# A two-layer hybrid trunk: a new order of steps, gate rows in memory of their own, quarter-size products, and another division of the opening adaLN work

## The chip, the cores and the metric

The kernel runs on 1 core of one Trainium2 chip. The metric is the device time in microseconds of one launch. Shown is the median of three runs; beside it stands one profiled execution, from which all rows are taken. The engines are TensorE (PE; its weight loads are shown as PEld), VectorE (DVE), ScalarE (ACT), GpSimd (POOL) and SyncE (SP, which here only issues transfers).

## The reference

Two layers work on x of 512 tokens by 1024 channels, batch 1, float32. Cut to what matters here:

```python
mod = silu(c) @ ada_w + ada_b               # 1024 -> 3 x 1024, once per layer
shift, scale, gate = split(mod, 3)
h = rms_norm(x, norm_g) * (1 + scale) + shift
proj = h @ w_in                             # 1024 -> 8008 columns, three mixers and their gates
ya = hgrn2(q, f, i, lower_bound) * silu(hg_g)          # gated linear recurrence, chunks
yb = sparse_attention(q, k, v, indexer) * silu(at_g)   # relu indexer, top 128 of 512 keys
yc = s5(u) * silu(s5_g)                                # complex diagonal scan, GLU
merged = sum_n sigmoid(merge_g[n]) * (y[n] @ w_branch[n])
x = x + gate * (merged @ w_out)             # next layer
```

Within the recurrence the scores of a block of 128 tokens are `q_t . k_s * decay(s, t)` for s before t. The kernel builds them by levels m = 1, 2, 4, ..., 64: level m gives the pairs with s in the first half and t in the second half of a group of 2m tokens.

## The kernel before

Every weight matrix comes in chunks of 128 x 1024 floats (512 KB), 170 of them through a ring `raw` of four slots. A product keeps float32 precision by three fast matmuls (L1687 to L1689): both operands are split in a high part (`w_hi`, `h_hi`, made by ACT, L800 and L860) and a low part (`w_lo` by POOL in two halves, L766 and L767; `h_lo` by DVE, L1359). One chunk is 24 such matmuls of 512 columns. All others (transposes, recurrence levels, attention, column sums) are plain float32, which shows as two records a matmul. `w_hi` and `w_lo` have three slots each, so the split of a chunk waits until PE is through with the chunk three before.

`schedule()` writes one list of steps, STEPS, by hand. Each of the five engines walks the same list and issues its own part of each step, with semaphores between them; an engine never overtakes in its own part. The position of a step in the list is thus its place in five queues. SP looks ahead: at each step it first sends the weight chunks up to three past that step. ACT and POOL look ahead by `split_upto(step)`. PE's list is `tensor_order()`, which puts the column matmuls of adaLN a few chunks later than the step they belong to.

Steps that matter here:

- `xT`, `hs`: x is transposed to channels by tokens, and the mean square of each token is summed over the channels on PE by a matrix of ones (L1770 for layer 0, L1777 for layer 1, in quarters); ACT turns it to `rb`, 1 / rms (L849, L851).
- `ad0`, `ad1`, `md0` (layer 0, four blocks b of 256 channels): the scale part is made on PE as a row (`weight_row`, L1699, one weight column, eight matmuls of 256 columns), copied by ACT to `row` (L827) and turned to columns by PE (`to_columns`, L1706). The shift part is summed on DVE over eight slices (`ada_sum`, L1151 and L1153, each waiting for the one before) and added over partitions by PE with a column of ones (L1742). `md0` adds the bias (L1316, L1317) and makes 1 + scale times norm_g (L1320).
- `hk` (l, b): DVE makes x times scale times rb (L1355), ACT adds the shift and rounds to `h_hi` (L860), DVE makes `h_lo` (L1359). Then `tm iq` b, the first product of the layer (one chunk, 24 matmuls of 512 columns), can run on channels 2b and 2b+1.
- `ada`: 24 half chunks of the modulation of layer 0's gate and of layer 1's scale and shift, summed on DVE (L1153) from three slots in the arena that SP fills one step ahead; PE adds them over partitions (L1763). `mod` finishes them.
- `adp`, `adr`: layer 1's gate as rows on PE (L1699) from two chunks each, 0 and 1 at the border, 2 and 3 among the indexer's steps of layer 1. These eight chunks go through the same ring `raw`, and a slot is free again when PE has used it.
- `hg` (g, part): the recurrence for a pair of heads. Part 0 is the diagonal, parts 1 to 7 the levels (PE L1875; DVE's running products L1504 and its masked copy of the bank into `sct`, L1526), 8 and 9 the chunk states, 10 the output, 11 and 12 the norm. `topk` rounds (L1446, L1449) run on DVE between them.
- `s5`, `s5t`, `gelu`: the S5 branch; in part 2 DVE scans (L1263 to L1277), in part 3 PE turns the result (L1950).
- The border between the layers is the end of the list for layer 0: `wo` products, `hs`, the last `ada`, `adp` 0 and 1, `mod`, then layer 1's `hk`.

The functions that the change touches:

## Time and profile before

| | |
|---|---|
| Median of 3 runs | 1290.11 us (1287.2 to 1292.71) |
| The profiled execution, device time | 1287.9 us |
| Its span | 1286.1 us |
| PE busy | 1250.2 us, 97% |
| PEld busy | 1007.7 us, 78% |
| DVE busy | 870.4 us, 68% |
| ACT busy | 516.5 us, 40% |
| POOL busy | 497.7 us, 39% |
| Mean granted TensorE clock | 0.996 |

Busy time is the time in which at least one instruction of the engine runs. PE's ends are modelled, so back-to-back matmuls overlap in the rows (a 512-column one shows 0.39 us and the next starts 0.23 us later); starts are the numbers to go by. An idle time in square brackets names what ended it.

### The profile page before, as it was taken

The numbers are of one execution on the slowest core, as the hardware profiler recorded it, in microseconds if no ns is written. First come the engines' busy times: TensorE is split into PE (matmuls) and PEld (weight loads), VectorE is DVE, ScalarE is ACT, GpSimd is POOL, SyncE is SP. The second block draws the span as 40 slices with busy tenths as digits, with TensorE's granted clock in tenths as the row PEclk, the third lists the DMA queues.
The fourth block names the chain that finished last, engine by engine and source line by source line (L and its number), as shares of the span: only waits on it lengthen the run. The fifth ranks groups of instructions, "written<-read, shape, count | busy, mean of one in ns | idle before, by whom it ended". The sixth has DMA issues, their size and how long they took to land.

```text
span 1286.1 us, 16449 instructions
## 1 busy us (share of the span) xinstructions
PE 1250.2 (97%) x6240; PEld 1007.7 (78%) x6240; DVE 870.4 (68%) x1364; ACT 516.5 (40%) x858; POOL 497.7 (39%) x344
## 2 busy tenths in 40 slices
PE   7899999999999999999989999999999999999998
PEld 4687788887778878888748767888787888888887
DVE  5777886976587856777478468879656888544242
ACT  5253323763444333333233532256544443433331
POOL 1253243343544333555315322422444434255551
PEclk9999999999999999999989999999999999999999
DMA  9442111132234325473444221212321432244322
GB/s 354 145 162 69 64 53 63 54 127 66 66 92 113 103 75 209 157 254 100 165 158 169 75 107 50 66 52 64 131 66 50 140 99 68 75 150 162 98 82 66
DMA packets 63439, 142.04 MB, mean 110 GB/s; under 512 B 29440, under 2 KB 31616, under 8 KB 62592
## 3 DMA queue, kind: packets, MB, share of 16 engines
q1 hardware_dynamic: 54016, 137.84, 32.8%
q10 hardware_dynamic: 9344, 3.15, 1.0%
q8 instruction: 50, 0.82, 0.3%
q14 instruction: 29, 0.24, 0.1%
HBM read 128.12 MB, written 10.49 MB: 108 GB/s over the span
## 4 chain that ended last, share of the span: by engine, by line
PE 86%; DVE 5%; ACT 3%; DMA 2%; issue 2%; SPq 1%; POOL 0%; ACTq 0%; DVEq 0%
PE bank L1687 22%; PE bank L1689 22%; PE bank L1688 22%; PE bank L1875 4%; DMA raw<-in_wfull 2%; PE bank L1836 2%; PE bank L1860 1%; PE bank L1846 1%; SPq L721 1%; PE bank L1945 1%; PE bank L1699 1%; PE bank L1959 1%; PE bank L1958 1%; DVE h_lo L1359 1%; PE bank L1711 1%
## 5 line engine op out<-in xcount | busy, mean ns | idle before, releaser
L766 POOL TENSOR_TENSOR w_lo<-raw,w_hi 128x512 fp32r<-128x512 f32 (+1 forms) x170 | 241.2, 1419 | 769.0 <-ACT w_hi L800 769.0
L1687 PE MATMUL bank<-h_hi,w_hi 128*128 128x512 f32 x896 | 363.0, 405 | 2.1 <-ACT arena L874 2.1
L1689 PE MATMUL bank<-h_hi,w_lo 128*128 128x512 f32 x896 | 349.5, 390 | 0.0
L1688 PE MATMUL bank<-h_lo,w_hi 128*128 128x512 f32 x896 | 348.8, 389 | 0.0
L800 ACT ACTIVATE w_hi<-raw 128x1024 fp32r<-128x1024 f32 (+2 forms) x170 | 178.4, 1052 | 266.3 <-PE bank L1689 205.7
L767 POOL TENSOR_TENSOR w_lo<-raw,w_hi 128x512 fp32r<-128x512 f32 (+2 forms) x170 | 264.0, 1553 | 0.0
L1687 PEld LDWEIGHTS bank<-h_hi,w_hi 128*128 128x128 f32 x896 | 168.3, 188 | 42.9 <-issue 8.3
L1688 PEld LDWEIGHTS bank<-h_lo,w_hi 128*128 128x128 f32 x896 | 168.4, 188 | 38.7 <-issue 5.3
L1689 PEld LDWEIGHTS bank<-h_hi,w_lo 128*128 128x128 f32 x896 | 168.1, 188 | 35.8
L1687 PE MATMUL bank<-w_hi,h_hi 128*128 128x512 f32 (+1 forms) x256 | 97.6, 381 | 8.1 <-DVE h_lo L1359 4.4
L1688 PE MATMUL bank<-w_lo,h_hi 128*128 128x512 f32 (+1 forms) x256 | 95.3, 372 | 0.0
L1689 PE MATMUL bank<-w_hi,h_lo 128*128 128x512 f32 (+1 forms) x256 | 95.2, 372 | 0.0
L1687 PE MATMUL bank<-y_hi,w_hi 128*128 128x512 f32 x224 | 89.0, 397 | 0.0
L1689 PE MATMUL bank<-y_hi,w_lo 128*128 128x512 f32 x224 | 87.3, 390 | 0.0
L1688 PE MATMUL bank<-y_lo,w_hi 128*128 128x512 f32 x224 | 87.2, 389 | 0.0
L1153 DVE SCALAR_TENSOR_TENSOR ada<-arena,cs,ada 128x256 f32<-128x256 f32 x112 | 79.7, 711 | 6.4 <-DMA arena<-in_wada 2.5
L1875 PEld LDWEIGHTS bank<-arena 128*128 128x128 f32 x512 | 60.2, 192 | 10.5 <-issue 9.2
L1504 DVE TENSOR_TENSOR arena<-arena 128x1024 f32<-128x1024 f32 x28 | 45.5, 1625 | 31.0 <-PE bank L1875 30.9
L1875 PE MATMUL bank<-arena 128*128 128x128 f32 x512 | 63.0, 278 | 1.4 <-ACT arena L903 1.4
L1687 PEld LDWEIGHTS bank<-w_hi,h_hi 128*128 128x128 f32 x256 | 48.5, 189 | 18.3 <-issue 9.6
L1689 PEld LDWEIGHTS bank<-w_hi,h_lo 128*128 128x128 f32 x256 | 48.4, 189 | 7.8
L1688 PEld LDWEIGHTS bank<-w_lo,h_hi 128*128 128x128 f32 x256 | 48.6, 190 | 7.0
(276 smaller groups left out, 1797.8 us busy)
## 6 DMA issues: line engine op xcount, KB each, us to landing
raw<-in_wfull SPq DMA_DIRECT2D x178, 512.0 KB, 3.6
arena<-in_wada SPq DMA_DIRECT2D x40, 512.0 KB, 6.7
x_scratch<-xm SPq DMA_DIRECT2D x2, 2048.0 KB, 8.4
arena<-x_scratch SPq DMA_DIRECT2D x2, 2048.0 KB, 9.5
arena<-in_x SPq DMA_DIRECT2D x4, 512.0 KB, 5.6
arena<-in_s5m SPq DMA_DIRECT2D x2, 1024.0 KB, 6.4
u_scratch<-arena ACTq DMA_DIRECT2D x4, 512.0 KB, 4.0
arena<-u_scratch SPq DMA_DIRECT2D x8, 256.0 KB, 3.3
```

The source lines that it names most:

```text
L721: sp.dma_start(mt2[j % 2][jj * GC:(jj + 1) * GC, :, jj * GC:P], kt[0:GC, :, 0:(CH - jj) * GC]).then_inc(mt_in, 16)
L766: nc.gpsimd.tensor_tensor(lo[:, :half], raw_chunk(n)[:, :half], hi[:, :half].bitcast(F32), ALU.subtract)
L767: nc.gpsimd.tensor_tensor(lo[:, half:], raw_chunk(n)[:, half:], hi[:, half:].bitcast(F32), ALU.subtract).then_inc(lo_done, 1)
L800: nc.scalar.activation(chunk_view(n, w_hi[:, m % SPLIT_SLOTS]), raw_chunk(n), ACT.Copy).then_inc(hi_done, 1)
L1153: ins = v.scalar_tensor_tensor(acc, weights_[:, kk], c_k, acc, ALU.mult, ALU.add)
L1359: v.scalar_tensor_tensor(h_lo[:, k], ht[:, k % 4], mod[:, l, k:k + 1], h_hi[:, k].bitcast(F32), ALU.add, ALU.subtract).then_inc(h_ready, 1)
L1504: return v.tensor_tensor(qk, qk, ends.broadcast_to([P, 2, S // m, m]), ALU.mult)
L1687: mm(out_, a_hi, b_hi, start=first, stop=False)
L1688: mm(out_, a_hi, b_lo, start=False, stop=False)
L1689: return mm(out_, a_lo, b_hi, start=False, stop=last)
L1836: mm(dst[:, 0:(b + 1) * P], iq_t[ps, h // 2, b * P:(b + 1) * P], ik_t[ps, 0:(b + 1) * P], start=True, stop=True).then_inc(full((step, 0)), 1)
L1875: last = mm(dst[:, cs_], hk[:, 2 * g + i, cs_], hq[:, 2 * g + i, cs_], start=True, stop=True)
```

## The change

The list of steps is new from end to end, and so are these parts:

- Begin of layer 0: DVE sums the scale (`mac`) in two accumulators in turn, one for each half of the input channels, in place in the loaded tiles; PE adds both over partitions (four column matmuls, `ad1`). PE makes the shift as a row (`ad0`), ACT copies it at the new step `adc`, PE turns it to columns. ACT's `h_hi` waits for the shift, DVE adds it after its two products. DVE makes the low parts of the first four chunks (`low`); POOL begins with the fifth. ACT's Sin for the rope tables moves from `ad0` 0 to `ad0` 2. SP sends the scale tiles ahead of the shift tiles, and masks, gains and S5 vectors after the fourth block, not the third.
- Layer 1's gate rows: the eight tiles are loaded into `gate_home` in the arena by a new SP step `gin`, no longer through `raw`; `adp` 0, 1 and 2 stand at the border, 3 at the begin of layer 1.
- The column matmuls and the loads of `ada` are steps of their own (`adm`, `adl`), and `tensor_order()` is gone.
- The last level of the recurrence (m = 64) is a 64 x 64 product per block of 128 instead of 128 x 128, and DVE copies that quarter instead of a masked copy of the whole.

The diff, cut to its core (of the new order only the lines that the prediction speaks of):

```diff
-    steps += [("hs", 0), ("ad0", 0), ("ad1", 0)]
+    steps += [("hs", 0), ("ad0", 0), ("mac", 0), ("low", 0), ("ad1", 0), ("adc", 0)]
...
-            steps += [("md0", 0), ("hk", 0, 0), ("ad0", 1)] + tm("iq", 0) + [("ad1", 1), ("md0", 1), ("hk", 0, 1), ("ad0", 2)]
-            steps += tm("iq", 1) + [("ad1", 2), ("md0", 2), ("hk", 0, 2), ("ad0", 3)] + tm("iq", 2)
-            steps += [("ad1", 3), ("md0", 3), ("hk", 0, 3), ("lb", 0), ("s5l", 0, 0)] + tm("iq", 3)
+            steps += [("md0", 0), ("hk", 0, 0), ("ad0", 1), ("mac", 1), ("low", 1)] + tm("iq", 0)
+            steps += [("ad1", 1), ("md0", 1), ("adc", 1), ("hk", 0, 1), ("ad0", 2), ("mac", 2), ("low", 2), ("mac", 3)] + tm("iq", 1)
+            steps += [("ad1", 2), ("md0", 2), ("adc", 2), ("hk", 0, 2), ("ad0", 3), ("ad1", 3), ("md0", 3), ("low", 3), ("adc", 3)] + tm("iq", 2)
+            steps += [("hk", 0, 3), ("lb", 0), ("s5l", 0, 0)] + tm("iq", 3)
...
-        steps += cm("wo", 3, 0) + cm("wo", 2, 1) + next_layer("hs", 1) + cm("wo", 3, 1) + more(1) + out_tiles(1, 0, 1) + more(5)
-        steps += next_layer("hs", 2) + next_layer("adp", 0) + next_layer("hs", 3) + next_layer("mod", 0) + next_layer("adp", 1)
+        steps += cm("wo", 2, 1) + rows(1) + more(1) + cm("wo", 3, 1) + next_layer("adp", 0) + fetch(2) + rows(2) + next_layer("hs", 1)
+        steps += more(1) + fetch(1) + out_tiles(1, 0) + more(4) + next_layer("adp", 1) + fetch(1) + next_layer("adp", 2) + rows(2)
+        steps += out_tiles(1, 1) + out_tiles(2, 0) + more(1) + next_layer("hs", 2, 3) + out_tiles(2, 1) + rows(1) + out_tiles(3, 0, 1)
+        steps += next_layer("mod", 0) + fetch(1)
...
+        steps += late("adp", 3) + rope("iq0") + rope("iq1") + late("adr", 0) + tm("kvi", 0) + rope("ik") + [("s5l", l, 1)] + late("adr", 1)
...
+        steps += hg(0, 9, 10) + hg(1, 8) + cm("hg", 0, 0) + top1(11) + rope("qn") + top1(12, 13) + hg(0, 11) + top1(14) + top(2) + top1(15)
+        steps += rope("qs") + hg(0, 12) + cm("hg", 0, 1) + hg(1, 9, 10) + gate("hg", 0, 0) + cm("hg", 1, 0) + rope("q0") + rope("q1")
...
+                if kind == "gin":
+                    p = step[2]
+                    sp.wait_ge(y_done, gate_no(l - 1, 2, 3) + 1)
+                    if p == 3:
+                        sp.wait_ge(mt_in, 16 * CH * NW * l)
+                    for kh in range(2):
+                        sp.dma_start(gate_home[2 * p + kh], wada[16 + len(ADA) + 2 * GATE_ROWS.index((l, p)) + kh].rearrange(
+                            "p (k w) -> p k w", k=KC)).then_inc(gate_in[p], 16)
...
+                if kind == "mac":
+                    b = step[1]
+                    dve.wait_ge(scale_in[b], 32)
+                    halves = [ad_in[4 * b + 2 + kh] for kh in range(2)]
+                    done = []
+                    for kk in range(KC):
+                        for kh in range(2):
+                            acc = halves[kh][:, 0]
+                            c_k = cs[:, 2, KC * kh + kk:KC * kh + kk + 1]
+                            if kk == 0:
+                                done.append(mark(v.tensor_scalar(acc, acc, c_k, None, ALU.mult)))
+                                continue
+                            after(done[2 * (kk - 1) + kh])
+                            ins = v.scalar_tensor_tensor(acc, halves[kh][:, kk], c_k, acc, ALU.mult, ALU.add)
...
+                if kind == "low":
+                    b = step[1]
+                    dve.wait_ge(hi_done, b + 1)
+                    v.tensor_tensor(chunk_view(b, w_lo[:, b % SPLIT_SLOTS]), raw_chunk(b),
+                                    chunk_view(b, w_hi[:, b % SPLIT_SLOTS]).bitcast(F32), ALU.subtract).then_inc(lo_done, 1)
...
-                    act.wait_ge(mod_ready, b + 1 if l == 0 else 4 + l)
+                    if l == 0:
+                        wait_read(act, (("adc", b), 0))
+                    else:
+                        act.wait_ge(mod_ready, l)
...
+                            if m == P // 2:
+                                half = [a.rearrange("p (c t) -> p c t", c=NT)[0:P // 2, :, P // 2:]
+                                        for a in (sct[:, 2 * g + i], banks[i][:])]
+                                v.tensor_copy(*half).then_inc(read((step, i)), 1)
+                                return
...
+                                if part == len(LEVELS):
+                                    first, second = slice(c * P, c * P + P // 2), slice(c * P + P // 2, (c + 1) * P)
+                                    last = mm(dst[0:P // 2, second], hk[:, 2 * g + i, first], hq[:, 2 * g + i, second],
+                                              start=True, stop=True)
+                                    continue
```

## Rows read from the trace of the kernel before

**Rows 1.** the page, busy time, share of the span and instructions

```profile
span 1286.1 us, 16449 instructions
...
PE 1250.2 (97%) x6240; PEld 1007.7 (78%) x6240; DVE 870.4 (68%) x1364; ACT 516.5 (40%) x858; POOL 497.7 (39%) x344
```

**Rows 2.** 25 us stretches: PE, PEld, DVE, ACT, POOL busy, clock, DMA, GB/s

```profile
50.00:75.00 25.00, 20.55 (x101) 17.57 (x102) 21.15 (x46) 8.64 (x14) 9.45 (x8) 0.93 0.35 127
...
650.00:675.00 25.00, 19.23 (x73) 10.32 (x73) 20.61 (x35) 10.32 (x14) 6.25 (x4) 0.86 0.58 200
...
875.00:900.00 25.00, 24.76 (x128) 20.35 (x127) 24.57 (x47) 14.53 (x20) 5.93 (x6) 1.00 0.22 64
```

**Rows 3.** waits of PE over the span: us, times, longest

```profile
PE bank L1763 <- DVE ada L1153: 5.2, 2, 4.3
...
PE bank L1950 <- DVE arena L1276: 3.7, 2, 2.2
...
PE bank L1687 <- ACT arena L881: 1.6, 2, 0.8
```

**Rows 4.** timeline of PE at the begin: start, us, then the instruction

```profile
29.00 0.47 PE L1687 MATMUL bank<-w_hi,h_hi 128*128 128x512 f32 x1 [0.72 <-DVE h_lo L1359]
...
39.44 0.47 PE L1687 MATMUL bank<-w_hi,h_hi 128*128 128x512 f32 x1
...
60.31 0.77 PE L1687 MATMUL bank<-w_hi,h_hi 128*128 128x512 f32 x1 [3.67 <-DVE h_lo L1359]
```

**Rows 5.** timeline of DVE at the begin

```profile
19.12 3.61 DVE L1153 SCALAR_TENSOR_TENSOR ada<-arena,cs,ada 128x256 f32<-128x256 f32 x7
...
25.83 1.42 DVE L1355 SCALAR_TENSOR_TENSOR arena<-xm,mod,arena 128x512 f32<-128x512 f32 x2
...
29.15 5.50 DVE L1153 SCALAR_TENSOR_TENSOR ada<-arena,cs,ada 128x256 f32<-128x256 f32 x7
```

**Rows 6.** timeline of POOL at the begin

```profile
29.04 1.29 POOL L766 TENSOR_TENSOR w_lo<-raw,w_hi 128x512 fp32r<-128x512 f32 x1 [3.26 <-ACT w_hi L800]
```

**Rows 7.** groups of DVE: busy, mean ns, idle before and releaser

```profile
L1504 DVE TENSOR_TENSOR arena<-arena 128x1024 f32<-128x1024 f32 x28 | 45.5, 1625 | 31.0 <-PE bank L1875 30.9
...
L1516 DVE TENSOR_TENSOR arena<-arena 128x1024 f32<-128x1024 f32 x4 | 4.9, 1222 | 0.1
```

**Rows 8.** timeline of PE at the border between the layers

```profile
650.30 3.61 PE L1699 MATMUL bank<-raw,cs 128*1 128x256 f32 x16
...
653.85 1.98 PE L1777 MATMUL bank<-arena,cst 128*128 128x512 f32 x4
...
661.94 1.01 PE L1763 MATMUL bank<-cst,ada 128*128 128x1 f32 x4 [4.25 <-DVE ada L1153]
...
662.88 6.00 PE L1699 MATMUL bank<-raw,cs 128*1 128x256 f32 x16
...
669.49 0.47 PE L1687 MATMUL bank<-w_hi,h_hi 128*128 128x512 f32 x1 [0.61 <-issue]
...
681.98 0.50 PE L1687 MATMUL bank<-w_hi,h_hi 128*128 128x512 f32 x1 [1.33 <-POOL w_lo L767]
```

**Rows 9.** timelines of ACT and DVE at the border

```profile
656.57 1.28 ACT L851 ACT_TABLE_LOAD   x1
...
663.15 1.06 ACT L800 ACTIVATE w_hi<-raw 128x1024 fp32r<-128x1024 f32 x1 [4.65 <-DMA raw<-in_wfull]
...
666.08 3.31 DVE L1359 SCALAR_TENSOR_TENSOR h_lo<-arena,mod,h_hi 128x512 fp32r<-128x512 f32 x2 [1.27 <-ACT h_hi L860]
```

**Rows 10.** timeline of PE, small plain products

```profile
168.16 2.05 PE L1875 MATMUL bank<-arena 128*128 128x128 f32 x16
...
466.95 3.74 PE L1945 MATMUL bank<-arena 128*128 128x64 f32 x32
```

**Rows 11.** groups of weight loads, by form

```profile
L1875 PEld LDWEIGHTS bank<-arena 128*128 128x128 f32 x512 | 60.2, 192 | 10.5 <-issue 9.2
...
L1929 PEld LDWEIGHTS bank<-arena 128*16 128x16 f32 x128 | 11.8, 97 | 4.2 <-issue 2.8
```

More of the change, by code:

```diff
@@ L70, in schedule, with taken, fetch, rows @@
         todo += [("ada", l + 1, c) for c in range(16)] if l + 1 < DEPTH else []
-        if todo:
-            todo.insert(12, ("mod", l, 16))
-        def more(n):
-            out = []
-            while todo and (n or todo[0][0] == "mod"):
-                n -= todo[0][0] == "ada"
-                out.append(todo.pop(0))
-            return out
+        fetches = [("adl", l, i) for i in range(len(todo))]
+        columns = [("adm", l, p) for p in range(len(todo) // 2)]
+        def taken(from_, n):
+            out = from_[:n]
+            del from_[:n]
+            return out
+        def more(n):
+            return taken(todo, n)
+        def fetch(n):
+            return taken(fetches, n)
+        def rows(n):
+            return taken(columns, n)
+        def first_gates():
+            return [("mod", 0, 16)] if l == 0 else []
         def tm(name, *cs_):
@@ new lines, in schedule @@
+        steps += load("yback", 2) + s5(3, 2) + tab(3, 3) + cm("wb1", 2) + s5(3, 3) + gelu(2, 0) + gelu(1, 1) + gelu(2, 1)
+        steps += cm("mg1", 3) + s5(3, 4) + load("ysave", 3) + fetch(2) + more(2) + gelu(0, 2, 3) + fetch(1) + cm("wb1", 3)
+        steps += cm("sg", 0, 0) + load("yback", 3) + more(1) + gelu(1, 2, 3) + cm("sg", 0, 1) + cm("sg", 1, 0) + gelu(3, 0) + gelu(2, 2)
+        steps += cm("sg", 1, 1) + gelu(2, 3) + gelu(3, 1, 2) + cm("mg2", 0, 0) + fetch(2) + more(1) + fetch(2) + more(1) + rows(1)
@@ L184, in chunks_of @@
     kind = step[0]
-    if kind == "adp":
-        return [ada_chunk(step[1], 16 + 2 * step[2] + kh) for kh in range(2)]
     if kind == "tm":
@@ L268, in done_after @@
     for step in STEPS:
-        if step[0] != "adp":
-            n += len(chunks_of(step))
+        n += len(chunks_of(step))
         done[step] = done[group_of(step)] = n
@@ L390, in split_upto @@
         return 0
-    if step[0] in ("ad0", "ad1", "md0", "hk") and DONE[step] < 4:
-        return DONE[step] + (step[0] != "ad0")
-    if step[:3] == ("tm", 0, "iq"):
-        return DONE[step] + 1
-    if step[0] == "hk" and step[1] or step[0] == "adp" and step[2] < 2 or step[0] == "hs" and step[2] > 1:
-        return DONE[step] + (step[0] == "hk" and step[2] > 0)
+    if step[0] == "low":
+        return step[1] + 1
+    if DONE[step] <= 4 and step[0] in ("ad0", "mac", "adc", "ad1", "md0", "hk"):
+        return 0
+    if step[:3] == ("tm", 0, "iq") and step[3] < 3:
+        return 0
     near = FIRST[step] + len(chunks_of(step)) + RAW_SLOTS
-    return min(DONE[step] + (3 if step[0] in ("gelu", "s5", "s5t") else 2), sum(n < near for n in SPLIT_CHUNK))
-SHIFTS = (0, 1, 2, 3)
+    return min(DONE[step] + (3 if step[0] in ("gelu", "s5", "s5t") else 2), near, len(CHUNKS))
 WARM = 8
-ADP_NO = {n: i for i, n in enumerate(n for n in range(len(CHUNKS)) if n not in SPLIT_NO)}
+FIRST_LOW = 4
 def program(nc, wfull, wada, x, cvec, pos, lblog, vecs, gains, s5v, s5m, consts, masks, out):
@@ L547, in program @@
         ad0_acc, adp_used = sem("ad0_acc"), sem("adp_used")
+        gate_in = [sem(f"gate{p}_in") for p in range(4)]
         shift_in = [sem(f"shift{b}_in") for b in range(4)]
@@ L677, in _ @@
             for b in range(4):
-                for i in range(4):
+                for i in (2, 3, 0, 1):
                     if 4 * b + i == 15:
```

226 lines of the change are left out of this document (92 added, 134 removed).

## The prediction

> **What bounds the kernel now.** First the page's busy shares and span: TensorE (PE) is busy 1250.2 of 1286.1 us, so all its idle time together is 35.9 us; DVE, the next, is busy 68% [rows 1]. The kernel gets faster only where PE has less to do, where a PE wait goes, or where PE's clock doesn't fall. Then busy time in stretches of 25 us: PE loses 4.5 us in 50:75 and 5.8 us in 650:675, each time at a lower granted clock (0.93, 0.86) [rows 2]; these are the start of layer 0 and the border between the layers. Last, the waits by PE: on DVE's adaLN sums 5.2 us, on DVE in the S5 scan 3.7 us, on ACT's bank copies 1.6 us [rows 3]. What is left is thin: DVE is at 24.6 of 25 us in 875:900 while PE still loses only 0.2 us there [rows 2].
>
> **The change, part by part, against the profiled execution (span 1286.1, device time 1287.9 us).**
>
> *Begin of layer 0.* Before, the four blocks b go in one rhythm: 24 matmuls of iq (5.5 us), then PE's adaLN work for the next block, then iq again; it starts at 29.00 and 39.44, a period of 10.44 us, which also holds a PE-made row of 3.6 us [rows 4]. The fourth block has no further row to hide behind, so PE waits 3.67 us and starts at 60.31 at the low clock; 25 us at a mean of 0.93 are 3.5 us at half speed, 1.7 us of work lost, part of it in the idle time itself, so I take 1.4 [rows 2, 4]. The last iq matmul is thus over at about 60.3 + 5.5 + 1.4 = 67.2.
> DVE's sum over eight slices is one dependent chain: 7 instructions take 3.61 us when alone (0.52 each with the semaphore), but 5.50 us when POOL makes a low part [rows 5]; POOL's first half stands at 29.04, exactly there [rows 6]. So a POOL low part costs DVE 1.9 us. After the change POOL makes none of the first four. DVE makes each itself, one 128x1024 instruction of 1.22 us (the row of that size, undisturbed) [rows 7], and its sum runs in two independent accumulators. A chained instruction costs 0.52; two independent ones 512 wide take 1.42 together, 0.7 each [rows 5], so one 256 wide is worth 0.35 to 0.52; I take 0.40, sum 3.1 us (ends 2.6 and 4.0).
> Now the clock of the new order. Block 0: sum 18.8 to 21.9, low part to 23.1; PE's row is over at 23.0, the four column matmuls at 23.9; scale 24.4, two products to 25.8, the shift added 25.95, ACT's high parts to 27.3, h_lo to 28.1: iq starts at 28.2 instead of 29.0. Block 1: DVE has sum and low part done at 28.1 + 3.1 + 1.2 = 32.4, PE finishes iq at 33.7 and the columns at 34.6; from there the chain is 4.4 us (0.4 scale, 1.4 products, 0.2 shift, 1.4 high, 0.8 low, 0.2 semaphores), while PE has row and columns of 4.1 us to do: iq at 39.0. The chain is 0.3 us longer than before, because ACT now waits for the shift. Block 2: DVE has two sums and one low part in the one window, 39.0 + 3.1 + 1.2 + 3.1 = 46.4, 1.8 us later than PE has the columns (44.5 + 0.9 less overlap); h_lo at 50.6; PE meanwhile makes the row for block 3, and its columns wait for ACT's copy, which stands behind a high part (1.06): iq at 51.9 instead of 49.9. Block 3 then has everything ready: iq at 57.4 with no wait and no low clock, over at 62.9. The gain is 67.2 - 62.9 = 4.3, taken as **-4.5** with rounding of the first step; with the slow sum (4.0) it is -2.7, with the fast one -5.3. ACT's two Sin and their table load move to block 2, where ACT has 5 us free. SP's queue sends scale before shift; both land in the same place in turn as before, and masks, gains and S5 vectors now wait for the last block's four loads, with nothing needing them before 56 us.
>
> *Border.* Before: last wo matmul 647.6, first iq matmul 669.49. In between PE makes two sums of squares (1.9 each), two gate rows (3.61, and 6.00 at the low clock) and waits 4.25 us for DVE's last adaLN sum [rows 8]. Then the high parts wait for weights, since the gate rows sit in the raw ring (ACT idle 4.65 us on DMA raw), and POOL's low parts fall on DVE's h_lo: two take 3.31 us, where two undisturbed ones of this size take 1.4 [rows 5, 9]. After the change the gate rows have memory of their own, so iq's first two chunks are split during the wo matmuls. But the gap gets more PE work: adp 0, 1, 2 (3 x 3.6), hs 1, 2, 3 (1.9 each), four column steps (0.5 each): 18.5 us, ending 666.1. These now end last: ACT's Ln and Exp around a table load of 1.28, 2.7 us -> 668.8 [rows 9], and 3.2 us from there to the first matmul (as 25.83 to 29.00 in block 0) -> 672.0 [rows 4, 5]. DVE's last two sums wait for a column step that stands behind adp 2 (661.7) and end at 665.7, below the other chain. PE is idle 5 us, so the low clock comes again: +1.5 -> 673.5. Moved in from elsewhere are hs 1 and adp 2, 1.9 + 3.6 = 5.5; net 668.0 against 669.5, -1.5. The wait on POOL at 681.98 (1.33) [rows 8] goes, because PE arrives later than POOL. adp 3 between iq and kvi covers layer 1's half of the wait for ACT's bank copies, 0.8 us [rows 3]. Together -3.6; taken **-3.5**. Ends: 0 (the row work ends last and the low clock lasts through a whole chunk) and -5 (no low clock).
>
> *Quarter products.* The last level of each head pair runs 64x64 instead of 128x128: 2 layers x 2 pairs x 2 heads x 4 chunks = 32 matmuls, 64 records, all on the PE path. A 128x128 record costs 0.112 us: 16 take 2.05 with the last one's tail; one with 64 moving columns but 128 weight columns costs the same (32 in 3.74) [rows 10]. So the moving side doesn't count, the weight load does. No row has 64 weight columns. A load of 16 takes 97 ns, one of 128 takes 192 [rows 11]; between them 64 comes to 131, 0.68 of 192, which makes 0.076 per record and -2.3 us. Ends: 0 (no gain) and half the time, -3.6, or -5 if 64 by 64 is cheaper still than either half. I take **-2.5**.
> The Trainium skill, "TensorE: Matmul & The Clock Gate", section "LDWEIGHTS (loading the stationary operand)", has the load go with the number of weight columns alone, columns divided by 1.2 in ns; as an estimate that is 53 ns less per record, -3.4 us, and a total of 1278.7. That 64 moving columns cost as much as 128 under 128 weight columns agrees with it.
> DVE's eight masked copies become plain ones of a quarter's size: that takes time off DVE only, 0 on the path.
>
> *The new order inside the layers.* SP's, ACT's, DVE's and PE's orders all move. Work is the same. PE's waits between 75 and 640 us and between 710 and 1125 are small, and 3.7 us of them are the S5 scan's [rows 3], where wb1's third chunk still is the only cover and DVE still waits for ACT's sine; gelu's sigmoid ahead of it costs ACT 0.6. Relu runs of five are broken up, which can give 1 to 2 us. On the other side recurrence parts 9 and 10 now follow each other directly on PE in both pairs. Taken **0**, ends -4 and +8.
>
> Sum: -4.5 - 3.5 - 2.5 + 0 = -10.5, so 1277.4 for an execution like the profiled one (1287.9), which lies 2.2 below the median of the runs shown (1290.1); on that median 1279.6. I give 1279.5.
>
> **Rivals.**
> A, DVE takes the place (1279.6 + 8 = 1287.6). With parts 9 and 10 adjacent, PE waits for states that DVE makes only after level 7's product (1.63 us [rows 7]) and copies: about 2 us at 4 places, +8. For it: DVE at 24.6 of 25 [rows 2]. Against: DVE waited 30.9 us for PE ahead of the 28 level products [rows 7], 1.1 us each, so it runs ahead of PE.
> B, the edits don't do what they say (1287.9). The slices of the sum stay at 0.52 and DVE's three jobs in block 2's window end last (-2.7), the border's 18.5 us of PE work with a long low clock costs 4 more (-3.5 + 4 = +0.5), and a quarter product costs what a whole one does (0). For: 6.00 against 3.61 for the same row of eight matmuls [rows 8]. Against: chunks split early save 1.9 us of DVE.
> C, the other side (1299). The new order puts DVE behind PE by more than the 1.1 us it is now ahead at the 28 level products; from that point each place makes PE wait. At 0.7 us a place beyond the slack it is 28 x 0.7 = +20: 1279.6 + 20 = 1299.6. For: the masked rounds of top-k are spread anew between the levels. Against: PE loses 0.2 us in DVE's fullest window [rows 2], and low parts and masked copies lighten DVE.
>
> **How the numbers follow.** Forecast 0.62, A 0.22, B 0.07, C 0.09. The forecast's own range is 1273 to 1284. The range given, 1271 to 1290, takes in A and B and the ends of begin, border and quarter products; C is left out. No change is within 0.5% (6.5 us), about what can be told here: 1283.6 to 1296.6. Faster 0.65, same 0.26, slower 0.09.
>
> **What would show it.** Right: iq starts near 28.2, 39, 52 and 57.4 with no wait and a clock of 1.0 in 50:75; no POOL work before 56; six adaLN sums after the last wo; first iq matmul of layer 1 at about 18 us behind hs 1, PE idle about 5 us before it, no POOL wait after; 64x64 records at 0.06 to 0.08. Wrong: PE waits above 1 us at the recurrence's state product or the level products, a level record still at 0.112, or a fourth iq start past 60.

## The result, and the profile after

The kernel after takes 1269.2 us (median of 4 runs, 1268.4 to 1269.9), the one before 1291.4 (4 runs, 1287.2 to 1292.7); the ratio is 0.983 [0.9813, 0.9846]. That is 22 us faster, where 10.5 were forecast, and below the range given. The profiled execution after has a span of 1268.1 us (device time 1269.9) against 1286.1 (1287.9), so the two traces account for 18.0 of the 22. Of the other 4.2, 3.5 come from the profiled execution before, which is at the fast end of its kernel: of 62 timed runs (medians by group 1289.4 to 1291.4) one lies below it. The begin below shows one reason. The last 0.8 is that the profiled execution after is the longest of its four. All medians here leave out three executions (1826 and 4473 us of `quarter_alone`, 7197 of `mtin3_earlier`); the 1.7 us that an expectation below names for `quarter_alone` counts two of them in.

The page after, busy time of the engines (to compare with [rows 1]). PE is idle for 21.2 us, where it was 35.9.

```profile
PE 1246.9 (98%) x6256; PEld 1006.5 (79%) x6256; DVE 847.7 (67%) x1368; ACT 518.4 (41%) x860; POOL 479.6 (38%) x336
```

Stretches of 25 us, columns as in [rows 2]: the low clock is gone at the begin and still there at the border.

```profile
50.00:75.00 25.00, 24.22 (x136) 21.14 (x135) 21.86 (x44) 12.81 (x20) 8.31 (x7) 1.00 0.48 169
650.00:675.00 25.00, 19.52 (x73) 13.75 (x72) 15.13 (x26) 12.38 (x16) 4.67 (x4) 0.86 0.25 84
475.00:500.00 25.00, 25.00 (x128) 21.29 (x127) 11.21 (x19) 9.29 (x12) 8.46 (x7) 1.00 0.48 168
```

PE's waits over the span of the kernel after, the largest first. Of [rows 3] the adaLN sums (5.2) and the S5 scan (3.7) are gone; a wait of 5.5 with no releaser is new, the border's. The one of 1.1 for w_lo lies in layer 0.

```profile
PE bank L1714 <- DMA lbt<-in_lblog: 5.8, 1, 5.8
PE bank L1691 <- issue: 5.5, 1, 5.5
PE bank L1691 <- POOL w_lo L747: 1.1, 1, 1.1
PE bank L1691 <- ACT arena L856: 1.1, 1, 1.1
PE bank L1691 <- ACT arena L863: 0.8, 1, 0.8
...
PE bank L1910 <- DVE arena L1528: 0.5, 2, 0.3
```

Since work moved between places, equal times of two traces don't compare. What compares is the time between the starts of the same weight chunks on PE, worked out from PE's timeline of each profile (us; L0, L1 the layer; wb0 is the start of attention, mg1 means its first chunk, with which the S5 part begins here, and wb1 3 the fourth chunk of wb1, behind it; the columns between before and after are experiments from below, their names cut short):

```
from - to                     before  quart_a middle_a  mtin3_l  old_mid  mtin3_e    after
first matmul - L0 kvi          62.96    65.16    64.49    64.48    58.82    59.07    58.83
L0 kvi - wb0 (recurrence)     198.94   197.98   199.96   198.92   197.86   197.84   197.88
L0 wb0 - mg1 (attention)      127.27   127.22   125.95   127.39   127.26   125.95   125.95
L0 mg1 - wb1 3 (S5)            99.41   101.03    96.86    96.99    99.50   100.56    96.86
L0 wb1 3 - last wo            147.79   147.67   147.80   148.29   147.26   146.42   146.42
last wo - L1 hq 1             124.72   125.47   127.22   125.34   120.11   122.97   122.93
L1 hq 1 - wb0                 138.07   137.04   136.70   138.09   137.03   134.87   134.86
L1 wb0 - mg1 (attention)      127.18   126.93   125.95   131.41   127.45   125.95   125.95
L1 mg1 - wb1 3 (S5)            98.71    98.88    96.89    98.33    99.95    98.58    96.86
L1 wb1 3 - end                150.76   150.76   150.89   150.77   150.76   150.89   150.89
```

From before to after: begin -4.1, S5 -2.6 and -1.8, attention -1.3 and -1.2. The four rows that are left (L0 kvi to wb0, wb1 3 to the last wo, from there to hq 1, hq 1 to wb0) make -7.4 together, of which 2.1 are the quarter products (below).

*Begin.* PE of the kernel after, the starts of iq's four chunks; and DVE while PE works on the second of them (a sum is one row of 2 and one of 6, the low part stands behind it; the fourth block's sum follows at 44.42 in the same form).

```profile
29.82 0.47 PE L1691 MATMUL bank<-w_hi,h_hi 128*128 128x512 f32 x1 [0.25 <-DVE h_lo L1358]
...
40.62 0.47 PE L1691 MATMUL bank<-w_hi,h_hi 128*128 128x512 f32 x1 [0.25 <-DVE h_lo L1358]
...
52.63 0.50 PE L1691 MATMUL bank<-w_hi,h_hi 128*128 128x512 f32 x1
...
58.20 0.39 PE L1691 MATMUL bank<-w_hi,h_hi 128*128 128x512 f32 x1
```
```profile
40.39 0.61 DVE L1294 TENSOR_SCALAR arena<-arena,cs 128x256 f32<-128x256 f32 x2
40.91 2.46 DVE L1297 SCALAR_TENSOR_TENSOR arena<-arena,cs 128x256 f32<-128x256 f32 x6
43.29 1.22 DVE L1305 TENSOR_TENSOR w_lo<-raw,w_hi 128x1024 fp32r<-128x1024 f32 x1
```

A sum takes 2.9 us (40.39 to 43.29; forecast 3.1), the fourth chunk follows the third without a wait, and kvi starts at 64.58.

*Border.* PE of the kernel after, from the last wo product:

```profile
637.32 3.61 PE L1702 MATMUL bank<-arena,cs 128*1 128x256 f32 x16
640.86 1.05 PE L1763 MATMUL bank<-cst,ada 128*128 128x1 f32 x8
641.77 1.96 PE L1777 MATMUL bank<-arena,cst 128*128 128x512 f32 x4
643.67 7.07 PE L1702 MATMUL bank<-arena,cs 128*1 128x256 f32 x32
650.66 1.05 PE L1763 MATMUL bank<-cst,ada 128*128 128x1 f32 x8
651.58 3.87 PE L1777 MATMUL bank<-arena,cst 128*128 128x512 f32 x8
655.36 0.61 PE L1763 MATMUL bank<-cst,ada 128*128 128x1 f32 x4
661.45 0.77 PE L1691 MATMUL bank<-w_hi,h_hi 128*128 128x512 f32 x1 [5.48 <-issue]
```

This is the forecast's chain: 18.5 us of PE work were expected and are there, then a wait (5 forecast, 5.5 measured), and the low clock (records of 0.63 us until 666.7, 0.39 after).

*Quarter products.* A group of 16 takes 1.15 us, where [rows 10] have 2.05. The kernel after, and the same place with full-size products (`full_last_level`, below):

```profile
212.16 1.15 PE L1877 MATMUL bank<-arena 128*64 128x64 f32 x16
213.23 1.60 PE L1898 MATMUL bank<-arena 128*128 128x128 f32 x12
```
```profile
212.43 1.95 PE L1870 MATMUL bank<-arena 128*128 128x128 f32 x16
214.21 1.50 PE L1888 MATMUL bank<-arena 128*128 128x128 f32 x12
```

By the starts, a quarter record follows the one before after 0.058 us instead of 0.112. But each group of 16 pays at its edges: its first record starts 0.32 us behind the one ahead of it (0.23 at full size), what follows it starts 0.15 behind its last (0.11), and the next one 0.21 behind that (0.11). A group thus saves 0.5 us and not 16 x 0.054 = 0.9; the four groups save 2.1 us.

### The profile page after: what moved, and what is told of

Read it like the earlier page. It is cut to its first block, busy times and chain, and to the rows that moved or that the text cites. A ratio compares the mean times of both kernels' runs of the same rounds, so it can differ in the third digit from the quotient of the medians.

```text
span 1268.1 us, 16483 instructions
## 1 busy us (share of the span) xinstructions
PE 1246.9 (98%) x6256; PEld 1006.5 (79%) x6256; DVE 847.7 (67%) x1368; ACT 518.4 (41%) x860; POOL 479.6 (38%) x336
## 4 chain that ended last, share of the span: by engine, by line
PE 95%; DVE 2%; issue 1%; ACT 1%; POOL 1%; DMA 0%; SPq 0%; ACTq 0%; DVEq 0%
PE bank L1691 24%; PE bank L1693 24%; PE bank L1692 24%; PE bank L1880 4%; PE bank L1950 2%; PE bank L1836 2%; PE bank L1702 2%; PE bank L1846 1%; PE bank L1860 1%; PE bank L1934 1%; PE bank L1964 1%; PE bank L1963 1%; PE bank L1714 1%; PE bank L1853 1%; PE bank L1941 1%
## 5 line engine op out<-in xcount | busy, mean ns | idle before, releaser
L746 POOL TENSOR_TENSOR w_lo<-raw,w_hi 128x512 fp32r<-128x512 f32 (+1 forms) x166 | 235.7, 1420 | 769.1 <-ACT w_hi L780 769.0
L747 POOL TENSOR_TENSOR w_lo<-raw,w_hi 128x512 fp32r<-128x512 f32 (+2 forms) x166 | 251.2, 1513 | 0.0
L1691 PEld LDWEIGHTS bank<-w_hi,h_hi 128*128 128x128 f32 x256 | 48.8, 190 | 18.4 <-issue 11.2
L1503 DVE TENSOR_TENSOR arena<-arena 128x1024 f32<-128x1024 f32 x28 | 38.1, 1360 | 37.1 <-PE bank L1880 18.7
L1880 PEld LDWEIGHTS bank<-arena 128*128 128x128 f32 x448 | 52.2, 192 | 6.7 <-issue 5.9
L1135 DVE SCALAR_TENSOR_TENSOR ada<-arena,cs,ada 128x256 f32<-128x256 f32 x84 | 51.7, 615 | 5.1 <-DMA arena<-in_wada 2.4
L1880 PE MATMUL bank<-arena 128*128 128x128 f32 x448 | 54.5, 278 | 0.0
```

The source lines that it names most:

```text
L746: nc.gpsimd.tensor_tensor(lo[:, :half], raw_chunk(n)[:, :half], hi[:, :half].bitcast(F32), ALU.subtract)
L747: nc.gpsimd.tensor_tensor(lo[:, half:], raw_chunk(n)[:, half:], hi[:, half:].bitcast(F32), ALU.subtract).then_inc(lo_done, 1)
L1135: ins = v.scalar_tensor_tensor(acc, weights_[:, kk], c_k, acc, ALU.mult, ALU.add)
L1503: return v.tensor_tensor(qk, qk, ends.broadcast_to([P, 2, S // m, m]), ALU.mult)
L1691: mm(out_, a_hi, b_hi, start=first, stop=False)
L1880: last = mm(dst[:, cs_], hk[:, 2 * g + i, cs_], hq[:, 2 * g + i, cs_], start=True, stop=True)
```

## The experiments

All times are medians; what is compared with the kernel after is compared with its 1269.2, from four runs. The kernel before, timed again in each group of experiments, moved by 2 us between the groups, so a difference to 1269.2 of less than that is shown only where the stages show it too.

**The middle alone, and put back.** `middle_alone`: the kernel before with

```
- kvi 0, ropes, kvi 1, adr 0, kvi 2, ... idx(1, 3), adp 2, ... mg1 3 1   (old order)
+ iq ropes, kvi 0, ik rope, kvi 1, adr 0, kvi 2, ... mg1 3              (new order, adp and adr as before)
```


> The kernel before with one part of the change alone: the new order of the steps between the iq product and the last chunk of mg1, in both layers (adp 2, adp 3 and the adr steps stay where they stood, in the middle). Theory 1: the forecast's term of 0 for the new order was the failed step; the gaps between TensorE's matmuls beyond their back-to-back time fall by about 5 us in the middle of layer 0 and by about 8 in that of layer 1, so this kernel is 8 to 12 us faster than before, near 1281. The two S5 waits behind L1950<-DVE (3.7 us before) are gone. Rival 2: the term of 0 was right and the gain came from begin, border and products, which are each larger than forecast: this kernel is within 2 us of before. Rival A of the forecast, recurrence parts 9 and 10 adjacent: a PE wait of about 2 us at four places, 8 us slower.

Measured 1285.7 us, ratio to before 0.9958 [0.9946, 0.997]: 5.2 faster, less than expected. In its profile both S5 waits are gone, attention is shorter by 1.3 and 1.2, and the recurrence of layer 0 is 1.0 us longer: PE's first output product of a head pair (part 10) waits for DVE's masked copy of the last level's scores. The new order has no weight chunk between the two (waits of PE):

```profile
PE bank L1906 <- DVE arena L1527: 2.0, 4, 0.8
```

`old_middle`: the kernel after with the old order there.

> The kernel after with the old order between kvi and the last chunk of mg1 put back (adp 3, adr 0 and adr 1 stay ahead of and behind kvi 0, as in the kernel after). Theory 1: it gives back what the new middle brought: 8 to 12 us slower than after, near 1279, ratio to before 0.991. Rival 2 (the middle is worth nothing): within 2 us of after, 0.983.

Measured 1280.5 us: 11.3 slower than after. So the new order is worth 5.2 in the old surroundings and 11.3 in the new: theory 1, and the forecast's 0 is refuted from both sides. The stages of the two profiles differ by 8.6 us only. Of the 6 us between 5.2 and 11.3 the quarter copies explain 1.5 (below), and PE's S5 waits, 5.3 us here against 3.7 before, about as much; the rest is open. Rival A's place is the right one, its price 2.0 us instead of 8; what PE waits for there is the copy of the last level, not the chunk states.

**The place of mtin 3.** `mtin3_later` (before) and `mtin3_earlier` (after) are the same move in opposite directions:

```
  before: ... s5(3, 1) + load("mtin", 3, 0, 1) + cm("mg1", 2, 1) + tab(3, 2) + s5(2, 4) ...
  after:  ... s5(3, 1) + cm("mg1", 2, 1) + tab(3, 2) + s5(2, 4) + load("mtin", 3, 0, 1) ...
```


> The kernel before with one move: the eight transfers of mtin 3 on SP's queue stand behind chunk mg1 2 1 and S5 part 4 of block 2 instead of ahead of it, as in the kernel after. Theory 1: these transfers held up the weight chunks behind them, so ACT's high part, its Sin table and DVE's states came late; both S5 waits of PE (2.4 and 1.3 us, one in each layer) go, 2.5 to 3.7 us faster than before. Rival: the wait belongs to the order of gelu and tables on ACT, which stays here: within 1 us of before, and the waits stand.

> The kernel after with one move undone: the eight transfers of mtin 3 stand on SP's queue ahead of chunk mg1 2 1 again, where the kernel before had them; all else stays. In the kernel before, the opposite move alone brought 4.3 us by the medians and took both waits of PE for S5's states away. Theory: the place of these transfers is the whole of the S5 waits, so they come back (2.4 us in layer 0, 1.7 to 2.9 in layer 1), 4 to 5 us slower than after, near 1273.8. Rival: the new order around it (table parts and sigmoid in other places) has given ACT and DVE enough room of its own, so that it is within 1 us of after; then the gain of the order in the kernel after has several roots.

Measured: `mtin3_later` 1286.6 us, 4.3 faster than before, ratio 0.9969 [0.9959, 0.998]; `mtin3_earlier` 1275.3 us, 6.1 slower than after. The place of the eight small transfers on SP's queue is the largest part of what the forecast missed. The chain in the kernel before, first SP, then ACT (L1006 is the Sin for the S5 states):

```profile
460.51 5.09 SPq L721 DMA_DIRECT2D arena<-arena  x8
465.64 0.59 SPq L673 DMA_DIRECT2D raw<-in_wfull  x1
```
```profile
470.18 1.06 ACT L800 ACTIVATE w_hi<-raw 128x1024 fp32r<-128x1024 f32 x1 [5.46 <-DMA raw<-in_wfull]
```

The same in `mtin3_earlier`:

```profile
453.55 5.08 SPq L701 DMA_DIRECT2D arena<-arena  x8
458.67 0.97 SPq L647 DMA_DIRECT2D raw<-in_wfull  x1
```
```profile
462.92 1.06 ACT L780 ACTIVATE w_hi<-raw 128x1024 fp32r<-128x1024 f32 x1 [4.56 <-DMA raw<-in_wfull]
...
465.00 1.28 ACT L988 ACT_TABLE_LOAD   x1
466.29 0.63 ACT L988 ACTIVATE arena<-arena 128x512 f32<-128x512 f32 x1
```

SP has sent nothing since 439.9: it waits 13.5 us for ACT to make what the eight transfers carry, then takes 5.1 us to issue the eight. The weight chunk behind them is sent at 458.7; in the kernel after it is sent at 440.8, ahead of them. ACT waits 4.6 us for it, and the Sin for the S5 states (L988) stands behind that high part in ACT's queue. In the kernel after the same rows are, SP first:

```profile
454.56 5.95 SPq L701 DMA_DIRECT2D arena<-arena  x8
461.70 0.33 SPq L705 DMA_DIRECT2D y_scratch<-arena  x1
```
```profile
458.54 1.06 ACT L780 ACTIVATE w_hi<-raw 128x1024 fp32r<-128x1024 f32 x1
...
463.51 0.63 ACT L988 ACTIVATE arena<-arena 128x512 f32<-128x512 f32 x1
```

No weight chunk stands behind the eight, the high part starts without a wait, and the Sin is 2.8 us earlier. PE's wait is then 0 instead of (waits of PE in `mtin3_earlier`, and 10 us of the same kernel; columns as in [rows 2])

```profile
PE bank L1955 <- DVE arena L1258: 3.3, 2, 1.8
```
```profile
470.00:480.00 10.00, 8.31 (x28) 6.23 (x29) 9.30 (x13) 3.53 (x5) 3.06 (x2) 0.83 0.31 116
```

The clock fell too. The stage S5 of layer 0 is 3.7 us longer (table), of layer 1 1.7, together 5.4 of the 6.1. In the profile of `mtin3_later` both old S5 waits are gone, but it is the longest of its twelve runs (1292.0): it has a wait of 4.0 us for another S5 state, in the attention row of layer 1 (131.4 us). ACT waits 8.0 us there for a weight chunk sent among two groups of four such transfers; the kernel before sends them at the same moments and waits 5.1. `old_middle` has 0.4 us of PE's wait at this place, the other profiles have none; why the chunk landed later stays open.

**The quarter products in both orders.** `quarter_alone` (before with them), `full_last_level` (after without them); q and k stand for the operands:

```
+ if part == len(LEVELS):  mm(dst[0:64, second], k[.., first], q[.., second])     # PE
+ if m == P // 2:          v.tensor_copy(*half)                                      # DVE
```


> The kernel before with the quarter products alone (TensorE 64 by 64, and DVE's plain copy of the quarter). All theories: 64 records at a spacing of 0.058 us as in the kernel after, where they took 0.112; 64 x 0.054 = 3.5 us faster than before. Theory 1 (the middle was mis-sized, the rest right): 3.5, ratio 0.997. Rival 2 (each of the other parts larger than forecast): 5 or more, as DVE's shorter copies also take PE's small waits away. If DVE then is late at the next level instead: under 2.

> The kernel after with the last level of the recurrence at full size again (128 by 128 on TensorE, the masked copy on DVE), in the new order. Quarter products alone gave 1.7 us to the kernel before by the medians, and in its profile only 1.0 of the 1.73 us of each layer. Theory 1, the part and the order need each other: in the new order the product of the state (recurrence part 11) stands directly behind, and DVE's full masked copies are late for it: 3.5 us for the records, and 0.5 to 1 us of waits at four places, 4 to 6 us slower than after, 1273.5 to 1275. Rival, both are worth the same in either order: 1.7 to 2.5 slower than after.

Measured: `quarter_alone` 1288.5 us, 2.4 faster, ratio 0.9981 [0.9971, 0.999]; `full_last_level` 1272.4, 3.2 slower than after. In the old order the recurrence shrinks by 1.0 us a layer, which is two groups at 0.5 us, so the 3.5 that all theories took was too much; in the new it shrinks by 1.8, the two groups and 0.7 of waiting. Without the quarter copies the output product waits as in `middle_alone` (here L1900, 2.0 us in four waits; after 0.5 in two):

```profile
PE bank L1900 <- DVE arena L1525: 2.0, 4, 0.8
```

So the two parts need each other, as theory 1 has it: the smaller copies save 1.5 us, but only in the new order. Its 4 to 6 us were too high, because it took the records at 3.5 instead of 2.1.

**Attention.** `old_attention`: after, with the old order from mg0 0 0 to su 1 1.

> The kernel after with the old order of attention, top-k rounds and su around chunks mg0 0 0 to su 1 1, all before and behind it as in the kernel after. With the whole old middle, this stage took 127.3 and 127.5 us instead of 125.95 (from wb0's first chunk to mg1 1 0). Theory: six stalls of 0.4 to 0.5 us of PE on ACT's and DVE's parts of attention in each layer come back, 1.3 to 1.5 a layer: 2.5 to 3 us slower than after, 1272. The S5 stage stays at 96.9 us. Rival: the S5 stage is disturbed as well, since att and tables stand differently: 4 or more.

Measured 1271.4 us, 2.2 slower. Attention is 0.9 and 1.2 us longer, S5 unchanged. The 2.5 to 3 expected were a little high. PE waits for ACT's part of attention again (L1861, 1.0 us in three); which move within the stage takes the waits away was not taken apart.

**The begin.** `low_on_pool` and `halves_one_by_one` each undo one way of making the sum shorter, `sum3_later` the place of the fourth sum:

```
low_on_pool:        - dve: v.tensor_tensor(w_lo, raw, w_hi, subtract)      + pool: the same in two halves
halves_one_by_one:  - for kk in range(KC): for kh in range(2):              + for kh in range(2): for kk in range(KC):
sum3_later:         - ("low", 2), ("mac", 3)] + tm("iq", 1)                + ("low", 2)] + tm("iq", 1) ... ("mac", 3), ("low", 3)] + tm("iq", 2)
                    (and ad1 3, md0 3, adc 3 behind iq's third chunk instead of ahead of it)
```


> The kernel after with the first four low parts made by POOL again, in two halves each, instead of by DVE. The forecast's reason (a low part on POOL slows a DVE sum that runs beside it, 1.9 us a sum of seven instructions): DVE saves 1.2 us a block but loses about as much or more in each sum; blocks 0 and 1 start 1 to 2 us later, 1 to 4 us slower than after in all. Rival, that slowing is covered by PE's own row and iq work from block 1 on: within 1 us of after; then DVE's taking over the low parts is worth nothing.

> The kernel after with the two halves of each scale sum one after the other instead of in turn: each instruction of DVE then waits for the one just before it. If the forecast's 0.52 us for a chained instruction and 0.40 for one in turn hold, each sum is 0.8 to 1 us longer; block 0 starts that much later, and block 2, where two sums and a low part stand in one window, 1.6 to 2 later: 2.4 to 3 us slower than after. Rival, the chain's waits cost nothing at 256 wide: within 0.5 us.

> The kernel after with the fourth block's scale sum, low part, columns and shift one window later: they stand ahead of and behind iq's third chunk, as the second block's stand around the first, instead of being made in the third block's window. Theory (the forecast's point): the fourth block then has no row of its own to hide behind, so PE waits about 3 to 4 us ahead of iq's fourth chunk and the granted clock falls; against it iq's third chunk can start earlier, by up to 1.2 us: 3 to 5 us slower than after, near 1273. Rival: the third window was too full (two sums and a low part), and it comes out within 1 us: then the gain of the begin lies in something else.

Measured: 1269.8, 1271.5 and 1274.9 us: 0.6, 2.3 and 5.7 slower than after. With POOL at its side, the second block's sum takes 5.0 us instead of 2.9 (DVE in `low_on_pool`, while PE works on the first chunk):

```profile
29.49 1.64 DVE L1292 TENSOR_SCALAR arena<-arena,cs 128x256 f32<-128x256 f32 x2
31.06 3.49 DVE L1295 SCALAR_TENSOR_TENSOR arena<-arena,cs 128x256 f32<-128x256 f32 x6
```

But DVE is then through at 34.5 and PE at 36. While PE works on the second chunk it is POOL that waits: the two sums take 2.9 us each, and POOL's instruction 4.67 instead of 1.3. The begin is 0.8 us longer by the stages; so the rival is right and the low parts are worth nearly nothing. With the halves one by one a sum takes 3.7 us, as expected; blocks 0 and 1 lose nothing by it, the third chunk comes 1.3 us later, and the begin is 1.2 us longer in the profile (the shortest of its runs). What counts is the fourth block. PE in `sum3_later`, and its stretch:

```profile
62.00 0.76 PE L1691 MATMUL bank<-w_hi,h_hi 128*128 128x512 f32 x1 [3.80 <-DVE h_lo L1358]
```
```profile
50.00:75.00 25.00, 20.16 (x94) 16.56 (x93) 20.13 (x46) 9.87 (x17) 6.91 (x6) 0.86 0.40 148
```

The same wait is in every kernel with the old begin, and in three of four it has this clock of 0.86; the profile before had 0.93 [rows 2]. This is one place where that execution was lucky: iq's first chunk to kvi took 39.3 us in it, 39.8 to 40.4 in the three others.

**The border, towards a faster version.** Seven kernels move adp 2, adp 3 and the two adr steps of the kernel after:

```
adp3_in_gap:          + adp 3 ahead of mod                       - adp 3 behind iq
adp3_gap_adr_iq:      the same, adr 0 behind iq 1, adr 1 behind iq 3
adp2_behind_squares:  adp 1, column, hs 2, hs 3, 2 columns, adp 2    - adp 1, adp 2, 2 columns, hs 2, hs 3, column
adp2_behind_adr0_iq:  the same, adr 0 behind iq 1
adp2_between:         adp 1, column, hs 2, hs 3, column, adp 2, column
adp23_in_gap:         the same + adp 3; ACT's copies of the gate rows in steps of their own, behind hk and behind iq 1;
                      adr 0 behind iq 0, adr 1 behind iq 3
copy_ahead_of_hk:     the same, the first copy ahead of hk
```


> The kernel after with one move meant to beat it: layer 1's last gate row (adp 3, 3.6 us of TensorE work) stands ahead of the step mod in the gap between the layers, where TensorE waits 5.5 us for the Ln, Exp and first products of layer 1, and no longer between iq and kvi. Theory: 3.6 us of work go into that wait, and with less than 2 us of idle time the granted clock stays up, which gives back another 1.5 to 2 us; against it stands 0.8 us of a bank wait that the row covered between iq and kvi: 4 to 5 us faster than after, near 1264.5. Rival 1: DVE's last sums or ACT's chain come later, because the column step and hs 2, 3 share a queue with the row: 2 us or less. Rival 2: the clock falls all the same, 2.8 us.

> adp 3 in the gap between the layers again, now with the two adr steps moved as well: adr 0 between chunks 1 and 2 of layer 1's iq, adr 1 between iq and the bank copies. With adp 3 alone in the gap, PE gave the 3.6 us back behind iq: 2.7 us waiting for ACT's copy of the gate row (which stood behind the copies of iq's banks) and 1.6 us at kvi. Theory: that copy is now early, so the wait of 2.7 is gone, and the chunks kvi are again covered by adr 1's columns: 2.5 to 3.5 us faster than after, near 1266. Rival: the end of iq to kvi is set by ACT's bank copies alone, whatever PE does in between; then no more than 1 us.

Measured 1269.0 and 1269.2 us: nothing. 3.6 us of work went into the wait, and PE gave them back, at the same instruction in both (waits of PE, `adp3_gap_adr_iq`):

```profile
PE bank L1709 <- ACT ada L814: 2.7, 1, 2.7
PE bank L1691 <- issue: 1.9, 1, 1.9
```

ACT's copy of the second gate row (in `adp3_in_gap`, of the first) stands behind its copies of iq's four banks, which wait for iq's end (ACT in `adp3_gap_adr_iq`), and PE now comes there first:

```profile
684.20 2.06 ACT L863 ACTIVATE arena<-bank 128x512 f32<-128x512 f32 x4 [4.35 <-PE bank L1693]
686.12 0.57 ACT L814 ACTIVATE ada<-bank 1x512 f32<-1x512 f32 x1
```

The wait of 1.9 ahead of iq is the same in both, but it lowered the clock only in `adp3_in_gap` (first row; the second is `adp3_gap_adr_iq`):

```profile
660.00:670.00 10.00, 9.27 (x34) 7.52 (x35) 8.85 (x13) 5.42 (x8) 0.39 (x1) 0.83 0.00 0
```
```profile
660.00:670.00 10.00, 9.06 (x40) 7.54 (x41) 9.06 (x14) 5.22 (x9) 0.18 (x1) 1.00 0.00 0
```

> The kernel after with adp 2 behind hs 2 and 3 and behind the last column steps, and the column step that DVE's last sum waits for directly behind adp 1. Nothing of ACT's Ln, Exp and DVE's first products hangs on adp 2, so they start 3.6 us earlier, and adp 2 lies in the wait of 5.5. By the rows of the kernel after: hs 3 is over at 651.6, Exp at 654.5, DVE's last sum at 653.1, mod at 654.7, the first iq matmul at 657.9 instead of 661.45. Theory: 3.5 us from that and about 1.9 from the clock, because PE is idle for 1 us or less: 5 us faster than after, near 1264. adp 3 still covers the bank wait. Rival 1: DVE's last sum is late since its slice arrives late: 1.5 to 3. Rival 2: the clock falls all the same: 3.5.

> As adp2_behind_squares, and adr 0 between chunks 1 and 2 of layer 1's iq. Its copy on ACT then stands ahead of the copies of iq's banks. Theory: adr 0's 0.9 us of PE work are no cover for anything, the copy costs ACT 0.5 us in either place: within 0.7 us of adp2_behind_squares. Rival: it takes ACT's time away from a high part that iq waits for, 0.5 to 1 slower; or it frees the bank copies 0.5 us earlier and is that much faster.

> As adp2_behind_squares, but adp 2 between the last two column steps. There PE waited 3.1 us for DVE's last sum, whose slices came 1.5 us late, and then made adp 2; iq started at 659.0 in a span that was 1263.2 long. Now adp 2 lies in that wait, the last column step comes at the same moment (653.3), and nothing is left between it and iq. Theory: iq's start is set by DVE's last sum and does not move, PE's idle time is the same 4 us, only in another place: within 1 us of adp2_behind_squares (1265.9). Rival: the clock is not lowered since no idle time stands ahead of a long row; 1.5 us faster.

Measured 1265.9, 1265.7 and 1266.6 us: 3.3, 3.5 and 2.6 faster than after; the second and third are within what was expected of the first. The first's own 5 us didn't come. The clock fell all the same (0.83 over 650 to 660), as rival 2 had it, and rival 1's cause holds: DVE's last sum waits twice for its slices, and PE for the sum (`adp2_behind_squares`, DVE):

```profile
648.64 0.35 DVE L1134 TENSOR_SCALAR ada<-arena,cs 128x256 f32<-128x256 f32 x1 [0.90 <-DMA arena<-in_wada]
...
651.19 2.04 DVE L1136 SCALAR_TENSOR_TENSOR ada<-arena,cs,ada 128x256 f32<-128x256 f32 x4 [0.64 <-DMA arena<-in_wada]
```

> As adp2_between, with adp 3 behind the last column step, and with the copies of both gate rows on ACT taken out of the queue behind iq: the first stands ahead of iq's first chunk, the second behind the second chunk; adr 0's columns stand behind iq's first chunk, adr 1's behind the fourth. Theory: PE has no idle time above 1 us between the layers, its clock stays up (1.5 us), and 3.6 us of row are hidden; against it 1 to 2 us of waiting for the copies of iq's banks, since only 0.9 us of columns cover them: 3 to 4 us faster than adp2_between, near 1262. Rival (adp 3 in the gap brought nothing twice): what lies behind iq takes it all back, 1265 to 1266.

> As adp23_in_gap, but ACT copies the first gate row ahead of its part of hk instead of behind it. There the copy stood at 666.5, behind ACT's last high part of hk, and PE waited 2.8 us for it behind iq's first chunk and then ran at the low clock for a while (0.77 in the 10 us that follow), while ACT had been idle for 2.97 us between Exp and its first high part. Theory: the copy fits into that idle time, the wait of 2.8 us goes and the clock stays: 3.5 to 4.5 us faster than adp23_in_gap, near 1263. Rival: what PE gains it loses at the next weight chunk or at the bank copies behind iq: less than 1.5.

Measured 1267.2 and 1261.4 us: the first missed its 1262 and is no faster than `adp2_between`, the second is 1.6 below the 1263 expected of it. In the first, PE waits 2.8 us for the first copy, which stands behind ACT's last part of hk, and then runs at the low clock. In the second ACT makes that copy while it waits for DVE. Its row, and the 10 us behind the gap:

```profile
656.29 0.59 ACT L815 ACTIVATE ada<-bank 1x512 f32<-1x512 f32 x1 [2.30 <-PE bank L1764]
```
```profile
660.00:670.00 10.00, 10.00 (x48) 8.14 (x48) 7.98 (x13) 6.38 (x9) 1.33 (x2) 1.00 0.00 0
```

`copy_ahead_of_hk` beats both kernels: ratio to before 0.9776 [0.9762, 0.979], 7.8 us below after.

## Why the forecast was wrong

Sizes are from the profiled executions, as in the forecast: 18.4 us between first and last matmul.

- *The new order inside the layers, 0: the step that failed.* Measured -6.9 (what is left of 18.4 after the other three): S5 -4.4, attention -2.5, recurrence 0 (layer 0 -1.1 from kvi to wb0, of which the quarter records are all; layer 1 the same once the 2.1 us that moved into the border are set aside). 1.5 of it need the quarter copies. By the runs it is 5.2 and 11.3. The forecast said that in the S5 part "wb1's third chunk still is the only cover and DVE still waits for ACT's sine". It looked at the cover on PE and at ACT's order, and did not ask why ACT was late: for a weight chunk that stood on SP's queue behind a step that first waits for ACT and then issues eight transfers (13.5 and 5.1 us in `mtin3_earlier`). The diff moves exactly these; the rule to count each DMA of a moved step had been applied at the begin, not here. The small waits in attention were passed over as thin; they come in both layers.
- *Begin, -4.5: -4.1* in the stage, -5.7 to -6.3 against the three other profiles with the old begin, where the clock fell further. The mechanism held (no wait at the fourth chunk, clock 1.00), its reasons did not weigh as said: POOL's slowing came in one window of two and costs 0.6 to 0.8, the fourth sum made early is worth 5.7. Block 0 gained nothing of the forecast 0.8 (24.1 us from the first matmul, before 23.7).
- *Border, -3.5: -5.3* (last wo to hq 1 -1.8; less 2.1 that the new order moved into this stage, as in layer 0 from kvi to hq 1; and -1.4 ahead of the last wo, where hs 1 left). The gap itself came out as forecast, 24.2 us from the last wo product's end to iq against 24.4. More was gained where adp 2, adp 3 and adr left: with adp 3 now counted ahead of kvi, the stage kvi to hq 1 is 8.3 us shorter, though 2.1 was moved in and the two rows are 7.2; a wait of 1.4 on ACT at a level product behind idx went, and half of the wait for the bank copies [rows 3]. The POOL wait at iq's second chunk is gone, as forecast [rows 8].
- *Quarter products, -2.5: -2.1* for the records, near the forecast by two errors that cancel. A record costs 0.058 us inside a group, where 0.076 was taken from the two rows at hand (97 and 192 ns put 64 columns at 138 ns and not 131, so 0.080 and -2.0); but the edges of the four groups, which no term counted, take back 1.3 us of the 3.4. The Trainium skill, "TensorE: Matmul & The Clock Gate", "LDWEIGHTS (loading the stationary operand)", makes a load go with its columns; the drop of 54 ns from 128 to 64 columns agrees with the 53 ns it gives. DVE's smaller copies were not worth 0: in the new order they take 1.5 us of waits away.
- *The base.* 3.5 us of the 22 are that the profiled execution before was among the fastest of its kernel: luck, not the change. The forecast knew 2.2 of it, and placed its sum on the median of three runs.
- *Rivals.* B's three failures didn't come, nor C's point (DVE behind PE at the levels). A's wait came at the named place, for the last level's copy, 0.5 us in the kernel after.

## What to carry to other kernels

When a wait ends on an engine's result, follow that engine's own lateness back to the queue that fed it before deciding that the wait stays; a step that waits, with a run of small transfers behind it, on the queue that also sends the weights is a candidate. Two edits that look independent (a new order, smaller operands) can need each other: the smaller copies here save 1.5 us in the new order and nothing in the old. A gap that has work put into it pays only if nothing behind it waits for a queue that did not move: look for copies that stand behind work which itself waits for PE.

## What the runs showed of the hardware

- A sum of eight 128x256 operations on DVE in two accumulators in turn takes 2.9 us, one half after the other 3.7 us. Beside POOL's 128x512 subtractions one of the two paid: once the sum took 5.0 us and POOL's two instructions 1.29 and 1.34, in the next window two sums took 2.9 each and POOL's instruction 4.67 (`low_on_pool`).
- Plain float32 records of 64 weight by 64 moving columns start 0.058 us apart, 128 by 128 ones 0.112; changing between the two sizes costs a group of 16 together 0.3 us at its edges.
- An idle PE of 3.7 us at the begin lowered the granted clock in all five profiles that have it, but to a different depth (0.93 once, 0.86 four times over the same 25 us). Shorter ones went either way at the same place: 1.9 us ahead of iq lowered it in `adp3_in_gap` (0.83 over 660 to 670) and not in `adp3_gap_adr_iq` (1.00); PE's first S5 wait lowered it in `quarter_alone` (2.3 us, 0.85 over 480 to 490) and not in the kernel before (2.2 us, 1.00). So the length of the wait alone does not decide.
- Issuing one small transfer cost SP 0.64 us (eight in 5.1; in the kernel after 5.9).
